# A two-layer hybrid decoder step on one core: the third token block's matmul operands made 128 rows high with zeros

## The chip, the cores and the metric

The kernel runs on one core of one Trainium2 chip. The metric is the device time of one execution in microseconds (us). Unchanged, it takes 1622.94 us, the median of three runs from 1620.73 to 1624.58.

## The reference

One inference step of a two-layer trunk on 256 prompt tokens and 64 sample tokens (8 sequences of 8), width 1024, all in float32. The kernel handles the 320 tokens in three blocks: 128, 128 and 64. Layer 0 mixes with four retention and four mLSTM heads and ends in a dense SwiGLU of width 2816; layer 1 mixes with eight HGRN2 heads and ends in two of eight SwiGLU experts. Cut to what matters here:

```python
def _retention(q, k, v, state):                      # per head and chunk
    intra = einsum('bhts,bhsv->bhtv', einsum('bhtk,bhsk->bhts', qc, kc) * decay, vc)
    inter = einsum('bhtk,bhkv->bhtv', qc, S) * q_dec
    S_new = S * chunk_dec + einsum('bhsk,bhsv->bhkv', kc * k_dec, vc)

def _mlstm(q, k, v, i_pre, log_f, C, n, m):
    s = einsum('bhtk,bhsk->bhts', qc, kc) * w
    num = einsum('bhts,bhsv->bhtv', s, vc) + w_prev[..., None] * einsum('bhtk,bhkv->bhtv', qc, C)
    den = sum(s, axis=-1) + w_prev * einsum('bhtk,bhk->bht', qc, n)
    n_new = dec[..., None] * n + einsum('bhsk,bhs->bhk', kc, w_end)

def _hgrn2(q, k, log_f, v, S):
    o = einsum('bhtk,bhkv->bhtv', qc * exp(A), S) + einsum('bhts,bhsv->bhtv', s, vc)

def _moe(h, w_router, b_router, wg, wu, wd):
    top_val, top_idx = top_k(einsum('bld,de->ble', h, w_router) + b_router, 2)
    gates = sum(one_hot(top_idx, 8) * softmax(top_val)[..., None], axis=-2)
    for e in range(8):
        out = out + gates[..., e:e + 1] * swiglu(h, wg[e], wu[e], wd[e])
```

## The kernel before

Each engine has its own instruction list, written in the order in which it runs, and semaphores tie the lists together. Activations are kept transposed, 128 features by 320 tokens. The mixers' order is written out by hand in two tables, `AB_STEPS` for layer 0 and `C_STEPS` for layer 1; every engine walks the same table and does its share of each step.

Where tokens have to be summed over, they lie on the partitions, and the three blocks of `BLK = [(0, 128), (128, 128), (256, 64)]` become three matmuls that contract over 128, 128 and 64 rows. Five places of that kind matter:

- `weigh` (L671 to L679), called by `outputs`: a head's values times the probabilities. L671 takes block 0, L672 block 1, L673 block 2 with 64 rows. Then come eight matmuls of 8 columns for the carried states (L679), or one against `ones` (L675) for the mLSTM denominator. It runs 20 times: 8 numerators and 4 denominators in layer 0, 8 numerators in layer 1. In some steps the pieces of a projection tile (L479 to L481) are woven between the state matmuls.
- `state_prompt` (L704 to L709): the new state of the prompt; L709 contracts the third block's keys over 64 rows against a mask of 8 columns, in four mLSTM heads.
- `state_samples` (L721): 32 rows high, eight instructions a head.
- `first_block` (L1046): gathers the tokens of expert 0's first round by a product of the token rows `HN` with a one-hot tile `ONE`, eight pieces of 128 features with three matmuls each, into two banks. ScalarE then rounds a bank to `xg_hi` (L1575), and VectorE computes the rest `xg_lo` (L2180).
- The loop over rounds follows. A round streams an expert's 35 weight units from HBM; ScalarE makes `w_hi` (L1568), VectorE `w_lo` (L2172), and TensorE multiplies (L479, L480, L481).

A float32 matmul in the program is two passes on the engine, each with a weight load (PEld) and a matmul (PE). So L673 is 40 of each in the trace and L1046 48 of each. Products in three float32r parts (L479 to L481) are one pass each.

Ahead of the loop VectorE's list has, in this order: the list of ranks and rows (to L2165), four units of `w_lo` (L2172), the gates (L2185 to L2193), and the two halves of `xg_lo` (L2180). `V` holds the values, `PB` and `PH` the probabilities of layer 0 and layer 1, `KN` the turned keys. All of these are regions of one large tile, `arena`, which the trace shows by that name; parts of it are used again for other things between the layers.

Of the kernel before, what the change touches and what calls it, by code (L numbers as in the profile page):

```python
# [15 lines left out]
P = 128  # L16
D = 1024
KD = D // P
TP = 256
NB, TS = 8, 8  # L20
SMP = NB * TS
NT = TP + SMP
BLK = [(0, 128), (128, 128), (256, 64)]
H4 = 4
HG = 8
DH = 128
# [23 lines left out]
CAP = 128  # L50
# [116 lines left out]
def trunk_kernel(nc, A, O):  # L167
    with ExitStack() as ctx:
# [5 lines left out]
        def S(name):  # L174
            if name not in sems:
                sems[name] = ctx.enter_context(nc.semaphore(name))
            return sems[name]

        banks = [ctx.enter_context(nc.psum_tensor(f"bank{i}", [P, 512], F32)) for i in range(8)]
# [23 lines left out]
        def C(name, rows=P):  # L203
            a, w = CONST[name]
            return cst[0:rows, a:a + w]
# [10 lines left out]
        ones = C("ones")  # L216

        def region(at, *shape):
            n = math.prod(shape)
            v = arena[:, at:at + n]  # L220
            if len(shape) == 1:
                return v
            if len(shape) == 2:
                return v.rearrange("p (a b) -> p a b", b=shape[1])
            return v.rearrange("p (a b c) -> p a b c", b=shape[1], c=shape[2])
# [6 lines left out]
        V = region(7680, 3, D)  # L232
# [5 lines left out]
        PB = region(21168, 2, 448)  # L238
# [11 lines left out]
        PH = region(23296, HG, 448)  # L250
# [22 lines left out]
        HN = region(4096, 3, D)  # L273
# [56 lines left out]
        WPS = small[:, 296:424].rearrange("p (a b) -> p a b", b=SMP)  # L330
# [33 lines left out]
        RTOK = sb("RTOK", [P, 3])  # L364
        HS = rows[0:KD, 0:2, :]
        XSQ = region(4352, D)
        ONE = region(8960, 3, CAP)

        DST = [ring[:, i * UNIT:(i + 1) * UNIT] for i in range(DSTAGE)]
        DWH = [parts(f"dense_hi_{i}", AT_RING + (DSTAGE + 2 * i) * UNIT, UNIT) for i in range(DSPLIT)]  # L370
# [74 lines left out]
        def _(pe):  # L445
            mm = nc.tensor.matmul
# [184 lines left out]
            for k in range(KD):  # L631
                b = open_bank("dve")
                for i, (t0, tn) in enumerate(BLK):
                    ins = nc.tensor.transpose(b[:, t0:t0 + tn], XN[0:tn, i, k * P:(k + 1) * P], ident[0:tn, 0:tn])
                close_bank("dve", ins, ("xT", k))
                if k == 3:
                    pe.wait_ge(S("prm_in"), 16 * 8)
                    b = open_bank("act")
                    ins = nc.tensor.transpose(b[:, 0:NPRM], PN[0:NPRM, :], ident[0:NPRM, 0:NPRM])
                    close_bank("act", ins, "prm")  # L640
            pe.wait_ge(S("token_scales"), 1)
            b = open_bank("dve")
            for i, (t0, tn) in enumerate(BLK):
                ins = mm(b[:, t0:t0 + tn], RS[0:tn, i:i + 1].to_broadcast([tn, P]), ident[0:tn, 0:tn], start=True, stop=True)
            close_bank("dve", ins, "n0_scale")
            pe.wait_ge(S("carry_in"), 32)
            b = open_bank("act")
# [21 lines left out]
            def weigh(b, left, probs, right, states, name, kind="dve"):  # L669

                mm(b[:, 0:TP], left(0), probs[:, 0:TP], start=True, stop=False, skip_group_check=True)  # L671
                mm(b[:, P:TP], left(1), probs[:, TP:TP + P], start=False, stop=False, skip_group_check=True)  # L672
                mm(b[:, TP:NT], left(2), probs[0:SMP, 384:448], start=False, stop=False, skip_group_check=True)  # L673
                if states is None:
                    ins = mm(b[:, TP:NT], ones, right, start=False, stop=True, skip_group_check=True)  # L675
                else:
                    yield
                    for s in range(NB):
                        ins = mm(b[:, TP + s * TS:TP + (s + 1) * TS], states[:, s, :], right[:, s * TS:(s + 1) * TS],  # L679
                                 start=False, stop=(s == NB - 1), skip_group_check=True)  # L680
                        if s % 2 and s < NB - 1:
                            yield
                close_bank(kind, ins, name)
                yield

            def outputs(layer, u, probs, probs_ready, right):
                values = lambda i: V[0:BLK[i][1], i, u * DH:(u + 1) * DH]
                probs_ready()
                pe.wait_ge(S(f"qe{layer}"), u // 4 + 1 if layer else u + 1)
                pe.wait_ge(S(f"state_in_{layer}_{u % NST}"), 16 * (u // NST + 1))  # L690
                kind = "act" if layer else "dve"
                b = open_bank(kind)
                yield from weigh(b, values, probs, right, ST[:, u % NST], ("num", layer, u), kind)
                if layer == 0 and u >= H4:
                    b = open_bank("dve")
                    pe.wait_ge(S("qn"), u - H4 + 1)
                    yield from weigh(b, lambda i: ones[0:BLK[i][1], :], probs, WPS[:, u % 2, :], None, ("den", u))

            def state_prompt(layer, u):
                after_empty(pe, ("kn", layer, u))  # L700
                kn = KN[:, u % 2]
                v = lambda i: V[0:BLK[i][1], i, u * DH:(u + 1) * DH]
                b = open_bank("act")
                mm(b[:, 0:DH], kn[:, 0, :], v(0), start=True, stop=False)  # L704
                ins = mm(b[:, 0:DH], kn[:, 1, :], v(1), start=False, stop=True)
                if layer == 0 and u >= H4:
                    mm(b[:, DH:DH + 1], kn[:, 0, :], ones[:, 0:1], start=True, stop=False)
                    mm(b[:, DH:DH + 1], kn[:, 1, :], ones[:, 0:1], start=False, stop=True)
                    ins = mm(b[:, DH + 1:DH + 9], kn[0:SMP, 2, :], C("bmask", SMP), start=True, stop=True)  # L709
                close_bank("act", ins, ("sp", layer, u))  # L710

            def state_samples(layer, u):
# [326 lines left out]
            def first_block():  # L1039

                pe.wait_ge(S("first_slots"), 3)
                for g in range(2):
                    for m in range(4):
                        at = slice((4 * g + m) * P, (4 * g + m + 1) * P)
                        for i, (t0, tn) in enumerate(BLK):
                            ins = mm(banks[g][:, m * CAP:(m + 1) * CAP], HN[0:tn, i, at], ONE[0:tn, i, :],  # L1046
                                     start=(i == 0), stop=(i == 2))
                    ins.then_inc(S("xg_full"), 1)

# [586 lines left out]
        def _(dve):  # L1636
# [15 lines left out]
                return bank_of(kind, n)  # L1652

            held = {"kind": "dve"}
            v.memset(rows[:, :, :], 0.0).then_inc(S("rows_zero"), 1)
            v.memset(wprow[:, :], 0.0).then_inc(S("rows_zero"), 1)

# [258 lines left out]
            def mix(src, tag, out, lo):  # L1916

                for u in range(KD):
                    if u == 2:
                        head_reciprocals(tag, 1)  # L1920
                    if u in HEADS[1]:
                        if tag == "hn1":
                            dve.wait_ge(S("gated1"), u + 1)
                        else:
                            after_empty(dve, ("cen", u))
                        scaled_head(src, tag, u)
                    low(out, u, src, lo)

            def projected_out(kind, tag, row, dst, lo=None, hi=None):
                for k in range(KD):  # L1930
                    add_to_x((kind, k), k)
                    after_empty(dve, (kind, k))
                    gained(tag, row, k, dst)
                    if k > 0 and lo is not None:
                        low(tag, k - 1, dst, lo, hi)
                    if k % 2:
                        split_dense()
                if lo is not None:
                    low(tag, KD - 1, dst, lo, hi)
                scale_of(tag)  # L1940
# [13 lines left out]
            for f in range(FT + 1):  # L1954
                if f < FT:
                    b = take(("fg", f))
                    free(v.tensor_tensor(SG[:, f % NSG, :], b[:, 0:NT], rsq[:, :], ALU.mult))
                if f == FT // 2:
                    for i in range(NST):
                        dve.wait_ge(S(f"state_out_{i}"), 16 * len(range(i, KD, NST)))  # L1960
                if f > 0:
                    dve.wait_ge(S("ff_hi"), f)
                    v.tensor_tensor(FTL[:, f - 1, :], SG[:, (f - 1) % NSG, :], FTH[:, f - 1, :].bitcast(F32),
                                    ALU.subtract).then_inc(S("ff_ready"), 1)
                if f < FT:
                    split_dense()
                    b = take(("fu", f))
                    dve.wait_ge(S("ff_silu"), f + 1)
                    free(v.tensor_tensor(SG[:, f % NSG, :], SG[:, f % NSG, :], b[:, 0:NT], ALU.mult))
# [71 lines left out]
            for name, u in C_STEPS:  # L2041
# [14 lines left out]
                elif name == "forget":  # L2056
                    forget(u)
                elif name == "scan":
                    dve.wait_ge(S("forget_ln"), u + 1)
                    for h in range(4):  # L2060
                        ins = v.tensor_tensor_scan(CUM[:, 4 * u + h, :], C("reset"), LV[u][1][:, h, :], 0.0, ALU.mult, ALU.add)
# [44 lines left out]
                                           op0=ALU.mult, op1=ALU.mult).then_inc(S("gated1"), 1)  # L2106
            after_fill(dve, ("lv", 1, 0))
            mix(OH, "hn1", "mix1", HL_O)
            projected_out("oc", "n3", 8, U_R)
            b = take("logit_rows")  # L2110
            dve.wait_ge(S("router_in"), 32)
# [277 lines left out]
```

## Time and profile before

| | before |
|---|---|
| median of 3 runs | 1622.94 us (1620.73 to 1624.58) |
| the profiled execution: time | 1626.39 us |
| its span, first to last instruction | 1624.6 us |
| TensorE busy | 1544.8 us, 95% |
| VectorE busy | 1167.6 us, 72% |
| ScalarE busy | 930.9 us, 57% |
| TensorE's mean granted clock | 0.965 of full |

The profiled execution is 3.45 us above the median of the runs, and its time is 1.8 us above its span. Busy TensorE time includes overlap of a pass with the next, so a stall of a tenth of a microsecond between passes can lie inside a stretch that counts as busy; it shows in the starts of the instructions.

### The profile page before, as it was taken

What the parts mean: (1) busy time and instruction counts of PE and PEld (TensorE: products, weight loads), DVE (VectorE), ACT (ScalarE), POOL (GpSimd) and SP (SyncE); (2) the same over time, 40 slices, a digit from 0 to 9 for tenths busy, and PEclk for the clock granted to TensorE, in tenths of its full rate; (3) what the DMA queues carried; (4) which work ended last, traced back from release to release, by engine and by line L of the source; (5) the groups of instructions that cost most, each with busy time, mean ns of one, the idle gap of its engine ahead of it and who ended that gap; (6) DMA issues with size and microseconds to landing.
All of it is one profiled execution on the core that took longest, in us unless ns stands there. A gap on an engine that the chain in (4) does not pass through costs nothing.

```text
span 1624.6 us, 23265 instructions
## 1 busy us (share of the span) xinstructions
PE 1544.8 (95%) x8656; PEld 1350.5 (83%) x8656; DVE 1167.6 (72%) x1256; ACT 930.9 (57%) x920; POOL 76.9 (5%) x90
## 2 busy tenths in 40 slices
PE   7999989999999989999989999999999999999994
PEld 5799778999999879986868888888888888888883
DVE  4755566555445696654468888888988888898887
ACT  4434544433334543333257786877778687777865
POOL 0012100000000000201020000000000000000001
PEclk9989999999999999977979999999999999999997
DMA  8567524797455422433189999999999999999983
GB/s 223 132 127 138 114 82 101 218 298 221 129 151 169 128 78 79 137 117 97 33 341 339 378 391 353 391 349 405 369 378 393 351 394 350 403 368 384 391 318 124
DMA packets 215874, 403.87 MB, mean 249 GB/s; under 512 B 15763, under 2 KB 132799, under 8 KB 215682
## 3 DMA queue, kind: packets, MB, share of 16 engines
q1 hardware_dynamic: 204400, 372.89, 66.7%
q0 software_dynamic: 6208, 22.06, 4.4%
q10 hardware_dynamic: 5202, 8.03, 1.5%
q8 instruction: 44, 0.72, 0.2%
q14 instruction: 20, 0.16, 0.0%
HBM read 372.65 MB, written 30.28 MB: 248 GB/s over the span
## 4 chain that ended last, share of the span: by engine, by line
PE 82%; DVE 8%; ACT 4%; issue 3%; DMA 2%; POOL 0%; ACTq 0%; SPq 0%; POOLq 0%; DVEq 0%
PE bank L479 24%; PE bank L480 23%; PE bank L481 23%; PE bank L679 2%; PE bank L936 1%; DVE dense_lo L1669 1%; PE bank L1075 1%; DVE w_lo L2172 1%; ACT dense_hi L1273 1%; PE bank L1046 1%; ACT w_hi L1568 1%; PE bank L721 1%; PE bank L584 1%; PE bank L671 1%; DVE arena L1778 1%
## 5 line engine op out<-in xcount | busy, mean ns | idle before, releaser
L2172 DVE TENSOR_TENSOR w_lo<-arena,w_hi 128x2048 fp32r<-128x2048 f32 (+1 forms) x284 | 606.4, 2169 | 104.0 <-ACT w_hi L1568 102.8
L1568 ACT ACTIVATE w_hi<-arena 128x2048 fp32r<-128x2048 f32 (+1 forms) x284 | 507.7, 1820 | 131.1 <-PE bank L481 118.6
L479 PE MATMUL bank<-w_hi,xg_hi 128*128 128x512 f32 (+1 forms) x768 | 288.0, 375 | 6.1 <-DVE w_lo L2172 4.7
L1669 DVE TENSOR_TENSOR dense_lo<-ring,dense_hi 128x2048 fp32r<-128x2048 f32 (+1 forms) x78 | 167.9, 2153 | 166.5 <-ACT dense_hi L1273 166.4
L480 PE MATMUL bank<-w_lo,xg_hi 128*128 128x512 f32 (+1 forms) x768 | 286.6, 373 | 0.0
L481 PE MATMUL bank<-w_hi,xg_lo 128*128 128x512 f32 (+1 forms) x768 | 285.8, 372 | 0.0
L1273 ACT ACTIVATE dense_hi<-ring 128x2048 fp32r<-128x2048 f32 (+1 forms) x78 | 140.6, 1803 | 161.1 <-PE bank L481 139.7
L479 PE MATMUL bank<-h_hi,dense_hi 128*128 128x320 f32 x512 | 171.9, 336 | 13.2 <-DVE h_lo_a L1675 5.2
L479 PEld LDWEIGHTS bank<-w_hi,xg_hi 128*128 128x128 f32 x768 | 144.9, 189 | 35.1 <-DVE w_lo L2172 7.6
L481 PEld LDWEIGHTS bank<-w_hi,xg_lo 128*128 128x128 f32 x768 | 144.5, 188 | 26.0
L480 PEld LDWEIGHTS bank<-w_lo,xg_hi 128*128 128x128 f32 x768 | 144.9, 189 | 25.0
L481 PE MATMUL bank<-h_hi,dense_lo 128*128 128x320 f32 x512 | 161.3, 315 | 0.0
L479 PE MATMUL bank<-w_hi,at_hi 128*128 128x512 f32 x352 | 139.3, 396 | 0.0
L481 PE MATMUL bank<-w_hi,at_lo 128*128 128x512 f32 x352 | 137.3, 390 | 0.0
L480 PE MATMUL bank<-w_lo,at_hi 128*128 128x512 f32 x352 | 137.0, 389 | 0.0
L479 PEld LDWEIGHTS bank<-h_hi,dense_hi 128*128 128x128 f32 x512 | 99.6, 195 | 24.4 <-issue 8.4
L479 PE MATMUL bank<-h_hi_f,dense_hi 128*128 128x320 f32 x352 | 109.5, 311 | 2.0 <-DVE h_lo_f L1675 1.9
L480 PE MATMUL bank<-h_lo_f,dense_hi 128*128 128x320 f32 x352 | 108.8, 309 | 0.0
L481 PE MATMUL bank<-h_hi_f,dense_lo 128*128 128x320 f32 x352 | 108.8, 309 | 0.0
L481 PEld LDWEIGHTS bank<-h_hi,dense_lo 128*128 128x128 f32 x512 | 99.5, 194 | 0.0
L480 PE MATMUL bank<-h_lo_a,dense_hi 128*128 128x320 f32 x256 | 81.4, 318 | 0.0
L481 PEld LDWEIGHTS bank<-w_hi,at_lo 128*128 128x128 f32 x352 | 66.1, 188 | 14.1
(391 smaller groups left out, 2376.4 us busy)
## 6 DMA issues: line engine op xcount, KB each, us to landing
arena<-in_w_moe_down SPq DMA_DIRECT2D x176, 512.0 KB, 6.3
arena<-in_w_moe_gate SPq DMA_DIRECT2D x128, 512.0 KB, 6.9
arena<-in_w_moe_up SPq DMA_DIRECT2D x128, 512.0 KB, 6.7
arena<-in_w_moe_gate SPq DMA_DIRECT2D x64, 384.0 KB, 4.1
arena<-in_w_moe_up SPq DMA_DIRECT2D x64, 384.0 KB, 3.8
ring<-in_w_in_ab SPq DMA_DIRECT2D x32, 512.0 KB, 9.0
ring<-in_w_in_c SPq DMA_DIRECT2D x32, 512.0 KB, 4.7
expert_rows<-ZERO SPq DMA_DIRECT2D x12, 1024.0 KB, 7.5
```

The source lines that it names most:

```text
L479: mm(out, left[0], right[0], start=start, stop=False)
L480: mm(out, left[0], right[1], start=False, stop=False)
L481: return mm(out, left[1], right[0], start=False, stop=stop)
L584: ins = mm(b[:, 0:NT], C("inv_d"), SQF[tag][:, k, :], start=(k == 0), stop=(k == KD - 1))
L671: mm(b[:, 0:TP], left(0), probs[:, 0:TP], start=True, stop=False, skip_group_check=True)
L679: ins = mm(b[:, TP + s * TS:TP + (s + 1) * TS], states[:, s, :], right[:, s * TS:(s + 1) * TS], start=False, stop=(s == NB - 1), skip_grou ...
L721: ins = mm(b[:, h * 256:(h + 1) * 256].rearrange("p (b v) -> p b v", v=DH), kn[rows_g, 2, :], VX[rows_g, at, :], start=True, stop=True)
L936: ins = mm(b[:, (2 * q + i) * P:(2 * q + i + 1) * P], L[:, h + q, at], L[:, h + q, at], start=True, stop=True)
L1273: fn(unit_flat(n, DWH), unit_flat(n, DST), ACT.Copy).then_inc(S("dense_hi"), 1)
L1568: fn(WH[SLOT_OF[p]][:, 0:unit_size(p)], STAGE[:, s, 0:unit_size(p)], ACT.Copy).then_inc(S("unit_hi"), 1)
L1669: v.tensor_tensor(unit_flat(n, DWL), unit_flat(n, DST), unit_flat(n, DWH).bitcast(F32), ALU.subtract).then_inc(S("dense_split"), 1)
L2172: v.tensor_tensor(WL[w][:, 0:n], STAGE[:, s, 0:n], WH[w][:, 0:n].bitcast(F32), ALU.subtract).then_inc(S("unit_split"), 1)
```

## The change

The third block's operands are taken 128 rows high in `weigh`, `outputs`, `state_prompt` and `first_block`. Rows 64 to 127 of the values, the probabilities, the token rows and the one-hot tile are set to zero by memsets on VectorE, so that the sums stay the same. The constant mask `bmask` already has zeros there. `state_samples`, the scores and the transposes stay as they were. `ONE` moves to another address, since the old one is still in use when its rows are set to zero.

```diff
-        ONE = region(8960, 3, CAP)
+        ONE = region(10240, 3, CAP)
...
-                mm(b[:, TP:NT], left(2), probs[0:SMP, 384:448], start=False, stop=False, skip_group_check=True)
+                mm(b[:, TP:NT], left(2), probs[:, 384:448], start=False, stop=False, skip_group_check=True)
...
             def outputs(layer, u, probs, probs_ready, right):
-                values = lambda i: V[0:BLK[i][1], i, u * DH:(u + 1) * DH]
+                values = lambda i: V[:, i, u * DH:(u + 1) * DH]
...
-                    yield from weigh(b, lambda i: ones[0:BLK[i][1], :], probs, WPS[:, u % 2, :], None, ("den", u))
+                    yield from weigh(b, lambda i: ones, probs, WPS[:, u % 2, :], None, ("den", u))
...
-                    ins = mm(b[:, DH + 1:DH + 9], kn[0:SMP, 2, :], C("bmask", SMP), start=True, stop=True)
+                    ins = mm(b[:, DH + 1:DH + 9], kn[:, 2, :], C("bmask"), start=True, stop=True)
...
                         for i, (t0, tn) in enumerate(BLK):
-                            ins = mm(banks[g][:, m * CAP:(m + 1) * CAP], HN[0:tn, i, at], ONE[0:tn, i, :],
+                            ins = mm(banks[g][:, m * CAP:(m + 1) * CAP], HN[:, i, at], ONE[:, i, :],
                                      start=(i == 0), stop=(i == 2))
...
+            def pad_values():
+                v.memset(V[SMP:P, 2, :], 0.0)
+
+            pad_values()
+            v.memset(PB[SMP:P, :, 384:448], 0.0)
             v.memset(rows[:, :, :], 0.0).then_inc(S("rows_zero"), 1)
...
                 if f == FT // 2:
+                    v.memset(PH[SMP:P, :, 384:448], 0.0)
...
                 elif name == "scan":
+                    if u == 0:
+                        pad_values()
                     dve.wait_ge(S("forget_ln"), u + 1)
...
             mix(OH, "hn1", "mix1", HL_O)
+            v.memset(HN[SMP:P, 2, :], 0.0)
+            v.memset(ONE[SMP:P, 2, :], 0.0)
             projected_out("oc", "n3", 8, U_R)
```

No instruction of TensorE, ScalarE, GpSimd or SyncE is added, dropped or moved; VectorE's list gets six memsets. Where they stand is seen in three pieces. Lines below the diff's first insertion carry higher numbers after it. The first piece is VectorE's list in layer 1 where the eight values are padded again, just ahead of the first scan (L2061 before, L2070 after); first the kernel before:

```order
L1990 TENSOR_SCALAR arena<-arena 128x320
L2047 TENSOR_TENSOR arena<-bank3,rsq 128x320
L1669 TENSOR_TENSOR dense_lo_0_71<-ring,dense_hi_0_69 128x2048
L2061 SCALAR_TENSOR_TENSOR arena<-cst,arena 128x320 x4
L1998 TENSOR_TENSOR arena<-arena 128x4x128
```

And the same place of the changed kernel:

```order
L1997 TENSOR_SCALAR arena<-arena 128x320
L2054 TENSOR_TENSOR arena<-bank3,rsq 128x320
L1675 TENSOR_TENSOR dense_lo_0_71<-ring,dense_hi_0_69 128x2048
L1657 MEMSET arena 64x1024
L2070 SCALAR_TENSOR_TENSOR arena<-cst,arena 128x320 x4
L2005 TENSOR_TENSOR arena<-arena 128x4x128
```

One memset of 64 rows by 1024 columns has come in between the split of a weight unit and the scan; nothing else moved.

The second piece is VectorE's list at the end of layer 1's mixer, behind the last head's `h_lo_o` and ahead of the first sum into `xT` (L1690 before, L1696 after). Before:

```order
L1849 TENSOR_TENSOR arena<-arena,bank2 128x320
L1675 TENSOR_TENSOR h_lo_o_54<-arena,h_hi_51 128x320
L1690 TENSOR_TENSOR xT<-xT,bank3 128x320
L1680 TENSOR_SCALAR cst<-xT,prm 128x320
L1690 TENSOR_TENSOR xT<-xT,bank4 128x320
```

After:

```order
L1855 TENSOR_TENSOR arena<-arena,bank2 128x320
L1681 TENSOR_TENSOR h_lo_o_54<-arena,h_hi_51 128x320
L2118 MEMSET arena 64x1024
L2119 MEMSET arena 64x128
L1696 TENSOR_TENSOR xT<-xT,bank3 128x320
L1686 TENSOR_SCALAR cst<-xT,prm 128x320
```

The memsets of the token rows and of the one-hot tile have come ahead of the first sum into `xT`.

TensorE's list at the first `weigh` reads the same in both kernels, since such a row shows the output's shape (128 by 64 for the third block) and not the height of the operands:

```order
L671 MATMUL bank5<-arena 128x256
L672 MATMUL bank5<-arena 128x128
L673 MATMUL bank5<-arena 128x64
L679 MATMUL bank5<-small,arena 128x8 x8
L658 MATMUL bank6<-arena 128x256
```

Only the height of L673's operands differs, 64 rows before and 128 after.

## Rows read from the trace of the kernel before

**Rows 1.** The page: TensorE's busy line, and the chain that ended last, by engine.
```profile
PE 1544.8 (95%) x8656; PEld 1350.5 (83%) x8656; DVE 1167.6 (72%) x1256; ACT 930.9 (57%) x920; POOL 76.9 (5%) x90
...
PE 82%; DVE 8%; ACT 4%; issue 3%; DMA 2%; POOL 0%; ACTq 0%; SPq 0%; POOLq 0%; DVEq 0%
```

**Rows 2.** Stage; us; busy (x) of PE, PEld, DVE, ACT, POOL; PE clock; DMA share; GB/s.
```profile
85.00:250.00 165.00, 154.16 (x968) 132.32 (x966) 100.51 (x222) 74.80 (x146) 28.33 (x39) 0.95 0.54 110
635.00:780.00 145.00, 139.59 (x858) 121.89 (x857) 85.81 (x171) 45.64 (x72) 19.35 (x20) 0.82 0.36 109
825.00:841.00 16.00, 14.88 (x48) 11.22 (x48) 12.15 (x19) 10.37 (x9) 8.62 (x6) 0.50 1.00 377
841.00:1600.00 759.00, 754.01 (x3611) 630.60 (x3612) 652.90 (x391) 575.26 (x422) 4.90 (x3) 1.00 0.96 365
```

**Rows 3.** Timeline of the gather's weight loads: start, us, instruction, form, count [idle before].
```profile
824.82 0.93 PEld L1046 LDWEIGHTS bank<-arena 128*128 128x128 f32 x4 [3.04 <-DVE RND L2160]
825.97 0.50 PEld L1046 LDWEIGHTS bank<-arena 64*128 64x128 f32 x2 [0.23 <-issue]
826.70 0.93 PEld L1046 LDWEIGHTS bank<-arena 128*128 128x128 f32 x4 [0.22 <-issue]
```

**Rows 4.** Timeline of TensorE at one `weigh` of layer 0, full clock.
```profile
100.53 0.38 PE L672 MATMUL bank<-arena 128*128 128x128 f32 x2
100.85 0.43 PE L673 MATMUL bank<-arena 64*128 64x64 f32 x2
101.21 1.95 PE L679 MATMUL bank<-small,arena 128*128 128x8 f32 x16
103.02 0.40 PE L479 MATMUL bank<-h_hi,dense_hi 128*128 128x320 f32 x1
```

**Rows 5.** The same at a `weigh` of layer 1 at half clock.
```profile
725.52 0.63 PE L672 MATMUL bank<-arena 128*128 128x128 f32 x2
...
726.71 2.09 PE L679 MATMUL bank<-arena 128*128 128x8 f32 x9
```

**Rows 6.** The chain in order of time: state matmuls behind `weigh`, and the gather.
```profile
87.13 1.88 PE bank L679 x16
...
720.63 3.51 PE bank L679 x16
...
753.63 3.51 PE bank L679 x16
```

**Rows 7.** VectorE and ScalarE at places where the chain leaves TensorE (timeline).
```profile
138.09 0.68 DVE L1778 SCALAR_TENSOR_TENSOR arena<-arena,bank 128x128 f32<-128x128 f32 x3 [1.15 <-PE bank L721]
...
709.09 0.49 DVE L2047 TENSOR_TENSOR arena<-bank,rsq 128x320 f32<-128x320 f32 x1 [0.94 <-PE bank L481]
```

**Rows 8.** Timeline of VectorE and ScalarE at the end of the gather.
```profile
839.24 0.69 DVE L2180 TENSOR_TENSOR xg_lo<-bank,xg_hi 128x512 fp32r<-128x512 f32 x1
840.55 0.69 DVE L2180 TENSOR_TENSOR xg_lo<-bank,xg_hi 128x512 fp32r<-128x512 f32 x1 [0.62 <-ACT xg_hi L1575]
...
835.01 0.58 ACT L1575 ACTIVATE xg_hi<-bank 128x512 fp32r<-128x512 f32 x1
839.92 0.60 ACT L1575 ACTIVATE xg_hi<-bank 128x512 fp32r<-128x512 f32 x1 [4.33 <-PE bank L1046]
```

**Rows 9.** VectorE where memsets come in (timeline): start, layer 1's scan, first sum.
```profile
1.22 1.66 DVE L1655 MEMSET rows<- 128x1920 f32 x1 [1.22 <-PEq L2381]
...
553.71 2.97 DVE L2061 TENSOR_TENSOR_SCAN arena<-cst,arena 128x320 f32<-128x320 f32 x4 [2.07 <-ACT arena L1518]
...
784.37 0.49 DVE L1690 TENSOR_TENSOR xT<-xT,bank 128x320 f32<-128x320 f32 x1 [0.81 <-PE bank L481]
```

**Rows 10.** VectorE at the start and in the dense SwiGLU (timeline).
```profile
9.99 0.49 DVE L1694 COPY xT<-bank 128x320 f32<-128x320 f32 x1 [7.03 <-PE bank L634]
...
380.31 2.29 DVE L1669 TENSOR_TENSOR dense_lo<-ring,dense_hi 128x2048 fp32r<-128x2048 f32 x1 [3.32 <-ACT dense_hi L1273]
```

**Rows 11.** Busy time and clock after the loop's start (windows).
```profile
846.00:850.00 4.00, 4.00 (x19) 3.31 (x18) 2.29 (x1) 3.19 (x2) 0.00 (x0) 1.00 0.05 18
```

## The prediction

> **What bounds the kernel now.** The page comes first: TensorE is busy for 95% of the span, and 82% of the chain that ended last is TensorE's [rows 1]. Then the busy time by stage. In both mixers and in the expert loop TensorE is busy for 93 to 99% of the stage. The gather ahead of the loop is the odd one: 48 passes fill 14.9 of 16 us, at a granted clock of 0.50, that is 1.2 GHz instead of 2.4 [rows 2]. The expert loop, 759 us, holds none of the changed matmuls.
>
> Next, the starts of the instructions around a change of height. In the gather, four loads with 128 rows follow each other inside 0.93 us, so each begins while the matmul before it runs. Then the engine's load side idles for 0.23 us, two loads with 64 rows come, and it idles for 0.22 us before the next with 128 rows [rows 3]. Columns, outputs and clock are the same on both sides; only the height differs. So a load whose height is not that of the matmul ahead waits until that matmul has drained, and one of the same height does not. The same is seen at the third block of `weigh` [rows 4, 5].
>
> **The gather, on TensorE.** One piece of 128 features is six passes, and the first two pieces begin at 824.82 and 826.70, 1.88 us apart [rows 3]; eight of them are the 15 us of the stage. A pass without a switch at this clock: 16 passes of the state matmuls take 3.51 us where they run without one [rows 6], 0.22 us each, so six are 1.32 us. That removes 0.56 us a piece, 4.4 us over eight pieces. The stage is then about 10.5 us instead of 15, and less if the denser work brings the clock up.
>
> **The gather, on the path.** Almost none of this reaches the end, because VectorE is late next. Its list has the weight parts and the gates ahead of `xg_lo`; it comes to the first half at 839.24 and to the second at 840.55, of which 0.62 us was a wait for ScalarE's second `xg_hi`, which had waited 4.33 us for the gather [rows 8]. With an early gather ScalarE does both halves back to back from 835.01 and is done by 836.2, and VectorE's second half follows its first without a gap. VectorE then ends about 0.65 us earlier, and so does the loop's start. Nothing else ahead of it depends on the gather. **Term: 0.65 us** (bounds: 0 if VectorE is held up elsewhere, 4.4 if I misread its list).
>
> **weigh, on TensorE.** From the first pass of L672 to the first of L679 are four passes: 0.68 us at full clock [rows 4]. Sixteen passes of L679 take from 101.21 to 103.02, 0.113 us each [rows 4]; four are 0.45 us, so 0.23 us goes. The pass behind the second switch starts slowly as well, which may add 0.02; I take 0.24. At half clock it is 1.19 us [rows 5] against 4 times 0.22, so 0.31 us goes. In the gather two loads with 64 rows fill 0.50 us and four with 128 rows 0.93 us [rows 3], which is one pace for both, 0.21 us for each further load; so the added rows cost no load time.
>
> There are 20 calls. In the chain, nine of the ten unwoven groups of 16 state matmuls appear, from 87.13 to 753.63 [rows 6], and the chain is on TensorE at the ten woven calls too; one call lies beside it. Three of the 19 on the chain run at half clock: there the 16 passes take 3.51 us instead of 1.88 [rows 6]. So 16 times 0.24 plus 3 times 0.31 is **4.8 us**. L709 switches from 128 to 64 rows and then to the 32 of L721; only the first switch goes, three of these four stand off the chain, and I put 0.1 us for all. L721's own switches stay.
>
> **How much of it passes.** Where the chain leaves TensorE, the other engine had been waiting for it: 0.94 and 1.15 us at the two tightest such places that I found [rows 7]. The matmul stretches between two such places hold two to four calls, 0.5 to 1.0 us of saving, just inside those waits. But the profile does not show waits that are nearly binding, and after a saving ScalarE's or VectorE's own list may be what ends some of them. I let 0.6 of the 4.9 us be lost: **4.3 us** passes (bounds: 2.0 and 4.9).
>
> **The memsets.** One of 128x1920 took 1.66 us, 0.86 ns a column [rows 9]; half the partitions may or may not be faster, and I take the same per column. The two at the program's start (1024 and 128 columns, 1.0 us) lie in the 7.03 us in which VectorE waits for the first transposes [rows 10]. The one in the dense SwiGLU (512 columns, 0.44 us) falls into a stage where VectorE waits 3.3 us in each step for a weight part [rows 10]. The one ahead of the scan (0.88 us) has 2.07 us of wait for ScalarE to fill [rows 9]. The two behind the mixer (1.0 us) stand where VectorE waits 0.81 us before the first sum [rows 9]; 0.2 us is not covered there, but TensorE has its next projection tiles to go on with. I cost all six at nothing. If none of this cover held, they would cost 3.3 us together.
>
> **The sum.** 4.3 + 0.65 is 5.0 us. Against the profiled execution of 1626.39 us that is 1621.4; it lies 3.45 us above the median of the runs, which would become 1617.9. I say **1618.0 us**, 0.31% below 1622.94. A difference of 0.2%, 3.2 us, is about what a measurement of this kernel can tell from no change.
>
> **Rival: the stalls go, the time stays (0.2).** Each saving is a quarter of a microsecond, and each could be eaten by the next wait. For it speaks that 18% of the chain is not TensorE's [rows 1] and that the largest single saving, the gather's, is already hidden. Against it the waits of 0.94 us and more at those places [rows 7]. With half the savings passed, 2.5 us, the time is 1620.5.
>
> **Rival: the height is not the cause (0.07).** Then the gaps stay and the time is 1623. What speaks for it: in `weigh` the number of columns changes too. What speaks against it: in the gather only the height changes [rows 3]. The Trainium skill ("TensorE: Matmul & The Clock Gate", section Part 3, "What overlaps and what doesn't") says that weight loads overlap running matmuls only when the row groups differ. By that rule 128-high operands behind 128-high ones could not overlap either, padding would remove nothing, and the sum would be zero. The trace does not agree: loads with 128 rows overlap each other there.
>
> **Rival: the clock turns it around (0.06), slower.** In the gather TensorE has only half the clock [rows 2], and has all of it by 846, 5 us into the loop [rows 11]. If the gather ends some 5 to 8 us earlier, the engine is idle until 840.6, and what the loop starts with could be a clock that comes back later than before. Each microsecond at half clock costs the loop half a microsecond. From 10 us more on, the 5.0 us are used up; with another 16 us like those of the gather [rows 2] the loss is 8 us, and the time is 1626. Against it: TensorE has no more waits in the loop than before, and in this trace the clock came back within 5 us of the loop's start, from an equally low state [rows 11].
>
> **A better case (0.1).** With the stalls gone, some of the stretches at half clock in layer 1 could go too. The stage's mean of 0.82 over 145 us means 52 us at half clock [rows 2], and a fifth less would give back 5 us: 1613.
>
> **How the numbers follow.** The forecast has 0.57, for 1616.4 to 1619.6. The range must take in the better case and most of the rival with half the savings: 1613.5 to 1622.0, which leaves out about 0.2 (the unchanged time, the slow clock, and the edge of the better case). Faster by over 0.2% means below 1619.7: the forecast and the better case give 0.67. Within 0.2% lie the half savings and the unchanged time, 0.27. Slower 0.06.
>
> **What would show it.** In the changed trace L1046's loads all have 128 rows and no idle time between them; 48 passes take 10.5 us or less. L672 to L679 take 0.45 us at full clock. ScalarE's two `xg_hi` stand back to back, the two halves of `xg_lo` do too, and the first L479 of the loop comes 0.65 us earlier in relation to VectorE's gates, with TensorE idle before it for 5 us or more. The expert loop looks as before. The prediction is wrong if the starts of passes in `weigh` still lie 0.68 us apart, if TensorE's waits in the mixers grow by what the passes lost, or if the stretches at half clock change by more than 5 us in sum.

## The result, and the profile after

The changed kernel took 1605.01 us (median of four runs, 1604.51 to 1605.55), before 1622.7 (four runs). The ratio is 0.9889 with a 95% interval of 0.9873 to 0.9905: 18 us less, where about 5 were forecast. In two later sets of rounds the same kernel came to 0.9905 and 0.9914, so 14 to 18 us is what it gains.

The page of the changed kernel: busy time, the granted clock in 40 slices, and the chain by engine.

```profile
PE 1516.5 (95%) x8656; PEld 1331.4 (83%) x8656; DVE 1171.1 (73%) x1262; ACT 931.1 (58%) x920; POOL 77.0 (5%) x90
...
PEclk9999989999999999988989999999999999999997
...
PE 81%; DVE 9%; ACT 4%; issue 3%; DMA 2%; POOL 0%; ACTq 0%; SPq 0%; POOLq 0%; DVEq 0%
```

The clock line of the kernel before, which was not shown ahead of the prediction:

```profile
PEclk9989999999999999977979999999999999999997
```

TensorE's share is that of [rows 1] and its part of the chain within one per cent of it, but TensorE is busy for 28 us less with the same 8656 passes. The clock lines say where to look: slices 3, 18, 19 and 21 of before are lower. Slice 6 is lower in the changed kernel, so the low places also move.

The stages of the changed kernel (same columns as [rows 2]), cut where the same work begins and ends: layer 0's mixer, layer 1's, the gather, the expert loop.

```profile
85.00:241.80 156.80, 146.45 (x968) 127.33 (x966) 100.51 (x222) 74.85 (x146) 29.40 (x39) 0.97 0.57 116
627.00:758.50 131.50, 125.00 (x854) 110.08 (x854) 85.84 (x171) 45.67 (x72) 19.38 (x20) 0.91 0.39 121
803.30:819.10 15.80, 8.07 (x49) 7.88 (x49) 12.47 (x20) 11.07 (x9) 8.63 (x6) 0.72 1.01 379
819.10:1578.00 758.90, 754.20 (x3614) 630.86 (x3615) 653.01 (x390) 574.92 (x421) 3.79 (x3) 1.00 0.96 365
```

Against [rows 2] layer 0's mixer is 8.2 us shorter and layer 1's 13.5; that is more than the 18 us of the medians because the profiled execution of before was a long one. VectorE's and ScalarE's busy times in them are the same to 0.1 us. The mean clock rose from 0.95 to 0.97 and from 0.82 to 0.91. The gather's stage is as long as before (15.8 against 16.0 us), since VectorE ends it, as forecast; TensorE's 48 passes fill 8 us of it instead of 15. The loop is the same.

TensorE's timeline at the `weigh` of [rows 4], in the changed kernel:

```profile
97.07 0.38 PE L672 MATMUL bank<-arena 128*128 128x128 f32 x2
97.29 0.33 PE L673 MATMUL bank<-arena 128*128 128x64 f32 x2
97.46 1.90 PE L679 MATMUL bank<-small,arena 128*128 128x8 f32 x16
```

From L672 to L679 it takes 0.39 us instead of 0.68: 0.29 us less, where 0.24 was forecast. A call of layer 1 at half clock, for [rows 5]:

```profile
709.10 0.63 PE L672 MATMUL bank<-arena 128*128 128x128 f32 x2
...
709.85 1.82 PE L679 MATMUL bank<-arena 128*128 128x8 f32 x8
```

Here it is 0.75 us instead of 1.19: 0.44 us less, where 0.31 was forecast. The weight loads of the gather, as in [rows 3]:

```profile
803.29 7.84 PEld L1046 LDWEIGHTS bank<-arena 128*128 128x128 f32 x48 [3.05 <-DVE RND L2171]
819.06 0.29 PEld L479 LDWEIGHTS bank<-w_hi,xg_hi 128*128 128x128 f32 x1 [7.92 <-DVE xg_lo L2191]
```

The 48 loads are one row now: no idle time between them, 7.84 us instead of 15. The first 4.7 us of them ran at a granted clock of 0.50 and the last 3.2 at 0.94 (windows). Behind them TensorE's load side waits 7.92 us for VectorE. ScalarE's and VectorE's rows at that place (timeline), for [rows 8]:

```profile
813.49 1.07 ACT L1575 ACTIVATE xg_hi<-bank 128x512 fp32r<-128x512 f32 x2
```

```profile
815.57 0.17 DVE L2196 TENSOR_TENSOR GATE<-GATE,arena 128x24 f32<-128x24 f32 x1
...
817.72 1.29 DVE L2191 TENSOR_TENSOR xg_lo<-bank,xg_hi 128x512 fp32r<-128x512 f32 x2
```

Both halves of `xg_hi` and of `xg_lo` stand back to back. VectorE is through with `xg_lo` 1.29 us after it begins, where before it took from 839.24 to 841.24: about 0.7 us less. The memsets, again on VectorE's timeline (start, before layer 1's scan, behind the mixer):

```profile
1.02 0.91 DVE L1657 MEMSET arena<- 64x1024 f32 x1 [1.02 <-PEq L2392]
...
543.69 0.91 DVE L1657 MEMSET arena<- 64x1024 f32 x1 [0.27 <-issue]
545.49 2.97 DVE L2070 TENSOR_TENSOR_SCAN arena<-cst,arena 128x320 f32<-128x320 f32 x4 [0.89 <-ACT arena L1518]
...
762.30 0.91 DVE L2118 MEMSET arena<- 64x1024 f32 x1 [0.27 <-issue]
763.19 0.17 DVE L2119 MEMSET arena<- 64x128 f32 x1
763.37 0.49 DVE L1696 TENSOR_TENSOR xT<-xT,bank 128x320 f32<-128x320 f32 x1
```

0.91 us each for 1024 columns; the scan still waits 0.89 us for ScalarE behind its memset.

So the savings that were counted out are there, and add up to about 6 us. The other 8 to 12 us need another source, and the clock lines point at the clock. One stretch as an example. First the kernel before, then the changed one, both from 88 to 112 us (windows, columns as above):

```profile
88.00:112.00 24.00, 24.00 (x137) 21.48 (x137) 12.52 (x31) 9.71 (x22) 3.58 (x8) 0.79 0.55 90
```

```profile
88.00:112.00 24.00, 23.56 (x167) 21.69 (x167) 17.70 (x43) 11.43 (x29) 5.19 (x9) 1.00 0.70 129
```

In the same 24 us the changed kernel makes 167 passes instead of 137. In the kernel before, one call of `weigh` lies in it and another call's third block just ahead of it, together worth 0.6 us of stalls. The clock was 0.79 of full and is 1.00. One stretch of one execution proves little, though: the same window is looked at in other runs below (e4).

### The profile page after: what moved, and what is told of

Its sections match the earlier page's. It is cut to its first block, busy times and chain, and to the rows that moved or that the text cites. A ratio compares the mean times of both kernels' runs of the same rounds, so it can differ in the third digit from the quotient of the medians.

```text
span 1602.7 us, 23271 instructions
## 1 busy us (share of the span) xinstructions
PE 1516.5 (95%) x8656; PEld 1331.4 (83%) x8656; DVE 1171.1 (73%) x1262; ACT 931.1 (58%) x920; POOL 77.0 (5%) x90
## 4 chain that ended last, share of the span: by engine, by line
PE 81%; DVE 9%; ACT 4%; issue 3%; DMA 2%; POOL 0%; ACTq 0%; SPq 0%; POOLq 0%; DVEq 0%
PE bank L479 24%; PE bank L480 23%; PE bank L481 23%; DVE w_lo L2183 2%; PE bank L679 2%; DVE dense_lo L1675 1%; PE bank L936 1%; PE bank L1075 1%; ACT dense_hi L1273 1%; ACT w_hi L1568 1%; PE bank L721 1%; PE bank L584 1%; DVE arena L1784 1%; PE bank L671 1%; PE bank L616 1%
```

## The experiments

The theory: each stall of a height change is short, but the stalls stand among thin matmuls (8 columns), and without them TensorE spends less time at the lower clock level (0.50 of full in the traces). The rival A: stalls alone, with the surplus from somewhere else (the gather, the memsets, the address of `ONE`). The rival B: it is the height of the third block itself, not the stalls, that the clock follows. In the expectations "Theory A" is the clock theory each time; "Theory B" is whatever other account that text names.

A measure for all runs is the time at half clock, 2 x (1 - clock) x span. It is given for the profiled execution and, since every execution's span and clock are known, as the mean of all runs. The second counts: within one kernel the executions differ by 6 us or so (standard deviation). Some 20 us of it in each run lie at the kernel's end.

| run | median us | ratio to before, interval | profiled span | clock | at half clock | the same, mean of all runs (runs) |
|---|---|---|---|---|---|---|
| before | 1622.7 | | 1624.6 | 0.965 | 114 | 107, 112, 109 (25, 19, 13) |
| changed | 1605.0 | 0.9889 (0.9873 to 0.9905) | 1602.7 | 0.976 | 77 | 77 (4) |
| e1, layer 0 alone | 1618.8 | 0.9972 (0.9952 to 0.9991) | 1620.6 | 0.965 | 113 | 102 (9) |
| e2, layer 1 alone | 1613.5 | 0.9935 (0.9905 to 0.9964) | 1615.1 | 0.970 | 97 | 90 (5) |
| e3, gather alone | 1621.9 | 0.9998 (0.9979 to 1.0018) | 1618.7 | 0.970 | 97 | 101 (10) |
| e4, before with added work | 1628.1 | 1.0041 (1.0023 to 1.0058) | 1624.4 | 0.972 | 91 | 98 (10) |
| e5, changed with switches | 1623.2 | 0.9994 (0.998 to 1.0008) | 1626.2 | 0.968 | 104 | 98 (10) |
| e6, changed, states too | 1609.9 | 0.9893 (0.987 to 0.9915) | 1609.1 | 0.977 | 74 | 67 (4) |
| e7, memsets alone | 1624.1 | 0.9993 (0.9982 to 1.0004) | 1623.6 | 0.963 | 120 | 111 (10) |
| e8, changed again | 1611.4 | 0.9905 (0.9887 to 0.9923) | 1610.2 | 0.971 | 93 | 87 (4) |
| e9, changed, control of e5 | 1612.3 | 0.9935 (0.9915 to 0.9956) | 1610.0 | 0.975 | 81 | 81 (6) |
| e10, changed, added work | 1612.6 | 0.995 (0.9932 to 0.9967) | 1610.0 | 0.974 | 84 | 79 (8) |
| e11, changed again | 1608.1 | 0.9914 (0.9886 to 0.9942) | 1609.8 | 0.972 | 90 | 80 (4) |

The kernel before had medians of 1620.49 beside e1 to e4, 1625.24 beside e5 to e8 and 1622.72 beside e9 to e11, with single runs from 1617 to 1628. So ratios are compared, not medians of different sets. These 57 runs also give the price of the clock, for they are one program, and their time at half clock goes from 97 to 124 us: a run with 1 us more of it is 0.38 us longer (the slope inside the three sets; 95% interval 0.32 to 0.43).

**e1, e2 and e3: the change in parts.** Each takes one part of the diff onto the kernel before: e1 the layer-0 half of `outputs` with `V` and `PB` set to zero, e2 the layer-1 half, e3 `first_block` with its two memsets.

```diff
-                values = lambda i: V[0:BLK[i][1], i, u * DH:(u + 1) * DH]
+                values = lambda i: V[0:(P if layer == 0 else BLK[i][1]), i, u * DH:(u + 1) * DH]
```

(and `layer == 1` in e2.)

> Only layer 0's weigh (8 numerators, 4 denominators) takes the third block 128 rows high; everything else as before. Theory A (clock): the passes saved at 12 switches are 12 times 0.29 = 3.5 us, and the two stretches at half clock before 110 us (10.2 us in the profile of before) go as well, which gives up to 5 us more: 8 us less than before in all, 1614.5. Theory B (stalls alone, the rest of the change's gain is from layer 1 or from elsewhere): 3.5 us less, 1619.

> Only layer 1's weigh (8 numerators) is 128 rows high. Theory A (clock): 8 switches pairs times 0.3 = 2.4 us, and some 20 us of half clock between 600 and 780 us go, worth 8 us more: 1612. Theory B (stalls alone): 2.4 us less, 1620.3. If the two layers add up, this run and the one of layer 0 together give the change's gain less 0.6 us for the gather.

> Only the gather of the first round is 128 rows high, with its two memsets. Both theories: the gather takes about 8 us instead of 15, the loop's start comes 0.65 us earlier in relation to VectorE's gates, the time is 0.65 us less, inside the noise: 1622. A rival that puts the change's surplus here (a loop that starts with a better clock) expects 5 us or more.

Measured: 0.28%, 0.65% and 0.02% less, that is 4.5, 10.5 and 0.3 us, in sum 15.4 us, as much as the whole change in e8. The eight calls of layer 1 gave more than twice what the twelve of layer 0 gave, with stalls worth only 2.4 us. e2 fits the clock theory (10.4 us) and not the stalls alone (2.4): its interval is 6 to 15 us, and it has 17 us less at half clock than before (90 against 107). e1 lies between 3.5 and 8, and its interval of 1.5 to 8 us doesn't decide; it has 5 us less at half clock. e3 takes the gather out as a source of 5 us or more: its 48 passes are done early, and the time is the same to within 3.4 us either way. It does have 6.5 us less at half clock (101 against 107). Its trace has 14 us of it around the gather where before had 20, a place where TensorE waits for VectorE anyway, so this part buys no time.

**e7: the memsets alone.** The changed kernel with all operands back at 64 rows.

> The six memsets and the moved one-hot tile of the change, with every matmul as before. All theories: the memsets lie in VectorE's waits and cost nothing, so the time is that of before within the noise. If they cost their own length it is 3.3 us more.

Ratio 0.9993, interval 0.9982 to 1.0004: nothing that can be told from no change. The memsets cost less than 1 us, and no more than 3 us of the gain can be theirs or the new address's. The time at half clock is that of before as well (111 against 112). With e3 this ends rival A as the source of the 8 to 12 us.

**e4: work added to the kernel before.** Two matmuls among the state matmuls of each numerator call:

```diff
                     for s in range(NB):
+                        if s in (0, 4):
+                            mm(b[:, NT:512], states[:, s, :], cst[:, CONST["cos"][0]:CONST["cos"][0] + 192],
+                               start=False, stop=False, skip_group_check=True)
                         ins = mm(b[:, TP + s * TS:TP + (s + 1) * TS], states[:, s, :], right[:, s * TS:(s + 1) * TS],
```

> The kernel before with all its 64-row matmuls, and two added matmuls of 192 columns per numerator call of weigh, into bank columns that nobody reads (16 calls, 32 matmuls, 64 passes of about 0.16 us at full clock, 10 us of work added; the result is unchanged). Theory A (clock): the added work fills the thin place behind the switches, the stretches at half clock in the mixers shrink from 75 us in sum to under 50, and the time rises by less than the 10 us added, or even falls: 1618 to 1628. Theory B (the clock has nothing to do with it): low stretches as before and about 9 to 10 us more, 1632.

The time rose by 0.41%, 6.6 us, for 10 us of added work: less than the work, as the clock theory had it. The median of 1628.06 is at the edge of that theory's range. The other account's 9 to 10 us lie at the upper end of the interval, 3.7 to 9.4 us. The clock decides more clearly: 98 us at half clock against 107 in the same rounds, 9.3 less (95% interval 3.5 to 15). At 0.38 us each that gives back 3.5 us, and 10 less 3.5 is what was measured. The window from 88 to 112 us of this run:

```profile
88.00:112.00 24.00, 24.00 (x168) 21.88 (x167) 14.25 (x31) 11.05 (x29) 5.13 (x10) 1.00 0.65 104
```

With all stalls left in, this stretch is at 1.00 instead of 0.79. But it is not fixed to one value either way. The same window of e3, which has all the stalls in layer 0, then of e9 (below), which has none:

```profile
88.00:112.00 24.00, 24.00 (x158) 22.07 (x158) 15.67 (x36) 11.07 (x28) 3.84 (x8) 0.93 0.64 118
```

```profile
88.00:112.00 24.00, 23.75 (x147) 21.30 (x147) 14.64 (x32) 10.98 (x27) 3.63 (x7) 0.86 0.57 92
```

Over all thirteen profiles: 0.79 in four with the stalls in layer 0 (before, e2, e5, e7) and 0.93 in e3; 1.00 in six without them (changed, e1, e6, e8, e10, e11) and 0.86 in e9; 1.00 in e4. So the stalls make the low place likely and do not settle it alone. With e4 the account is that the clock goes with how thickly TensorE's work lies; how it is granted in detail is not shown here.

**e5 and e9: the switches put back, and their control.** The changed kernel with one small matmul ahead of the third block in every call, 64 rows high in e5 and 128 in e9. The third block stays 128 rows high in both.

```diff
+                mm(b[:, NT:NT + 8], left(2)[0:SMP], probs[0:SMP, 384:392], start=False, stop=False, skip_group_check=True)
                 mm(b[:, TP:NT], left(2), probs[:, 384:448], start=False, stop=False, skip_group_check=True)
```

(e9 has `left(2), probs[:, 384:392]`.)

> The changed kernel, and in every weigh call one added matmul 64 rows high and 8 columns wide ahead of the third block, into bank columns that nobody reads; the result is unchanged. It brings back the two switches of height per call, while the third block itself stays 128 rows high. Direct cost: two passes of 0.11 us and 0.3 us of stalls, 20 calls, about 10 us. Theory A (the stalls are what costs the clock): the stretches at half clock in the mixers grow back towards the 75 us of before, and the time rises by more than the direct cost, to 1618 to 1626. Theory B (the clock follows the height of the third block's operands): low stretches stay near 44 us and the time is 1615.

> The control of the switch run: the changed kernel with the same added matmul of 8 columns per weigh call, but 128 rows high, so that the work is added and no switch. Direct cost: two passes of 0.11 us, 20 calls, 4.4 us. Theory A (the stalls cost the clock): the stretches at half clock in the mixers stay where the changed kernel has them (44 and 58 us in its two profiles), against 72 us in the switch run, and the time is 2 to 5 us above the changed kernel, 1608 to 1614. Theory B (any thin added matmul lowers the clock): low stretches and time as in the switch run, 1620 or more.

TensorE's timeline at one call of e5 (its L673 is the added matmul, L674 the third block, L680 the states):

```profile
102.50 0.38 PE L672 MATMUL bank<-arena 128*128 128x128 f32 x2
102.81 0.39 PE L673 MATMUL bank<-arena 64*128 64x8 f32 x2
103.13 0.43 PE L674 MATMUL bank<-arena 128*128 128x64 f32 x2
103.40 0.79 PE L680 MATMUL bank<-small,arena 128*128 128x8 f32 x6
```

And at the same call of e9:

```profile
100.09 0.38 PE L672 MATMUL bank<-arena 128*128 128x128 f32 x2
100.31 0.29 PE L673 MATMUL bank<-arena 128*128 128x8 f32 x2
100.45 0.41 PE L674 MATMUL bank<-arena 128*128 128x64 f32 x2
100.71 0.45 PE L680 MATMUL bank<-small,arena 128*128 128x8 f32 x3
```

0.90 us against 0.62 from L672 to L680: the same matmuls, and 0.28 us more only because one of them has another height. The weight loads of the added matmul, in e5 and then in e9, show it on the load side:

```profile
102.81 0.29 PEld L673 LDWEIGHTS bank<-arena 64*128 64x128 f32 x2
```

```profile
100.20 0.30 PEld L673 LDWEIGHTS bank<-arena 128*128 128x128 f32 x2
```

The first comes 0.31 us after the start of L672's matmuls, the second 0.11 us.

e5 is back at the time of before (0.9994), e9 kept most of the gain (0.9935). The added matmul itself has a part in that: e9 is 0.21%, 3.4 us, above e11, the changed kernel in the same rounds, near the 4.4 us expected. The height is the difference between e5 and e9, 0.59%, 9.6 us; the stalls on the path are 19 x 0.28 = 5.3 us of it. The two intervals are 0.14% and 0.2% wide to a side, so the rest, 4 us, is not certain from the times alone. The clock is clearer. e5 has 98 us at half clock (ten runs), 15 less than the kernel before in its rounds; e9 has 81 (six runs), 28 less than before in its own. That puts 13 us on the height (95% interval 7 to 19), worth 5 us at 0.38 each. The windows of e5, then of e9, from 600 to 680 us, in which layer 1's first `weigh` calls lie (e5 is some 9 us further back in its program there, so the work is not quite the same):

```profile
600.00:680.00 80.00, 72.75 (x551) 69.30 (x551) 57.43 (x108) 27.81 (x34) 7.70 (x6) 0.89 0.27 83
```

```profile
600.00:680.00 80.00, 75.46 (x605) 72.61 (x604) 58.18 (x111) 28.27 (x38) 11.83 (x10) 0.95 0.36 108
```

From 700 to 780 us it is 0.79 against 0.85. Rival B falls: the third block is 128 rows high in both, and with the stalls back more than half of the half-clock time that the change took from the mixers is back. In the traces the mixers have 72 us of it in e5 and 48 in e9, against 75, 65 and 78 in before, e3 and e7.

**e8 and e11: the changed kernel again.**

> The changed kernel once more, on the chip and in the rounds of these experiments, since the kernel before spread over 1617 to 1628 us here. If the result holds, it is 15 to 18 us below before.

> The changed kernel in the same rounds, to compare these two with: 13 to 18 us below the kernel before. Its stretches at half clock in the mixers are 40 to 60 us if the earlier two profiles were typical.

Both held, at 15 and 14 us. Their runs have 87 and 80 us at half clock on average, those of the first result 77, so the first result was the best of three.

**e6 and e10: is there more to have?** e6 pads `state_samples` as well, so that no height changes in the mixers' state work; e10 puts one added matmul of 192 columns per call into the changed kernel.

```diff
-        VX = region(14592, NB // 2, DH)
+        VX = region(14592, NB, DH)
...
-                        ins = mm(b[:, h * 256:(h + 1) * 256].rearrange("p (b v) -> p b v", v=DH), kn[rows_g, 2, :],
-                                 VX[rows_g, at, :], start=True, stop=True)
+                        ins = mm(b[:, h * 256:(h + 1) * 256].rearrange("p (b v) -> p b v", v=DH), kn[:, 2, :],
+                                 VX[:, at, :], start=True, stop=True)
```

> The changed kernel, and state_samples 128 rows high as well: eight column groups of values masked to their sequence instead of four, GpSimd's masking twice as wide. Trace of after: 16 heads have a switch from 128 to 32 rows and back, about 0.6 us of stalls at full clock, but the two 32-row groups also run side by side (8 passes of 256 columns in 1.07 us instead of 8 times 0.21). Direct effect: zero within 2 us. Theory A (the clock follows the stalls): fewer low stretches, 3 to 8 us less than the changed kernel, 1597 to 1602. Theory B: the time of the changed kernel, 1605.

> The changed kernel with one added matmul of 192 columns per numerator call among the state matmuls (16 calls, 5 us of work, result unchanged). If added dense work still buys clock once the stalls are gone, the low stretches in the mixers fall from about 50 us to 35 or less and the time falls by up to 3 us against the changed kernel of the same rounds. If what is left at half clock comes from waits for other engines, they stay near 50 and the time rises by 5 us.

e6 has the least time at half clock of all, 67 us in the mean, and yet 0.9893 against 0.9905 of e8 in the same rounds: the same within the intervals. The 3 to 8 us that the clock theory expected of it did not come. Its eight state passes no longer run side by side: at one head of layer 0 they take 1.89 us where they took 1.14. With 16 heads that can use up what the clock gave; that it did is not shown by a run of its own. e10 has 79 us against 80 in e11 and is 0.36% slower, 5.8 us, about its added work of 5 us. With the switches gone, added work bought nothing that these runs can show. Neither beats the changed kernel.

## Why the prediction was wrong

**The cause of the stalls: right.** A load whose height differs from that of the matmul ahead starts only about when that one is done (0.31 us behind its start, against 0.11); e5 and e9 show it with the height as the only difference. The rival that the height is not the cause falls. So does the rule that the prediction quoted for it from the Trainium skill ("TensorE: Matmul & The Clock Gate", Part 3, "What overlaps and what doesn't"), as far as these loads go: in the changed kernel 48 loads of 128 rows behind matmuls of 128 rows ran without idle time between them.

**The gather: right.** It took 7.84 us of loads (10.5 or less was forecast, "less if the denser work brings the clock up", which it did for the last 3.2 us), the loop started about 0.7 us earlier in relation to VectorE's gates (0.65), and TensorE waited for VectorE before it for 7.92 us ("5 us or more"). e3 found no measurable gain in it.

**weigh, on TensorE: a little small.** 0.29 us a call at full clock where I took 0.24. I gave every pass behind L672 the pace of the thin state passes, 0.113 us, and in the changed trace the four take 0.39 us. Over 19 calls this is 5.5 us instead of 4.8, and 6.0 with three calls at the 0.44 us that one at half clock saved.

**How much of it passes: nearly all, as far as the sum below shows.** No run measures it alone. VectorE's and ScalarE's busy times are unchanged stage by stage, and TensorE's nine largest waits for them from 85 to 780 us add up to 25 us before and 26 after.

**The memsets: right.** e7 leaves less than 1 us for them.

**The clock: the step that failed.** The sum is 4.3 us of stalls plus 0.65 us of the gather, with the clock at nothing. I had the mechanism, but only as "A better case (0.1)": "some of the stretches at half clock in layer 1 could go too", "a fifth less would give back 5 us". That was wrong in four ways. It was given one chance in ten when it was the likely course: every profile of the changed kernel shows fewer such stretches in the mixers (44, 58 and 55 us against 75, 65 and 78 in before, e3 and e7). It was looked for in layer 1 alone, while layer 0 had a low place as well, from 88 to 112 us, and lost it in all three. Its size was too small: in the first profile layer 1's stage has 24 us at half clock left of 52. And it was left out of the forecast's sum. The prediction's own sign of being wrong, "if the stretches at half clock change by more than 5 us in sum", came true.

The account, from all runs in the rounds of e8 and e11: the changed kernel's spans are 14 us shorter in the mean in both, with 26 and 29 us less at half clock. Some 6.5 of these are the gather's and buy nothing (e3), so about 20 are left. At the 0.38 us found inside the runs of the kernel before, they are worth 8 us; half a microsecond each would be the most, since half the clock is half the pace (3.51 us for the 16 passes that take 1.88 at full clock). The 6 us of stalls and gather make it 14. So the missing term measures about 8 us, more than the whole forecast of 5, and the range's lower end, 1613.5, was too high because of it.

**The slower rival** did not come: behind a 7.92 us wait the loop took 758.9 us, as long as before (759.0).

Why the twelve runs of the changed kernel have anything from 71 to 93 us at half clock is left open; it differs from execution to execution, and times with it.

## What to carry to other kernels

In a float32 stream of small matmuls, keep the operands' height the same from one to the next, with zeros if need be: a change to 64 rows and back costs 0.29 us at full clock here, and a full-height load takes no longer than a half-height one (0.19 us each). When TensorE's clock stands at half in a stage, price a small edit there twice: once for the stalls it removes, and once for the half-clock time that they may hold in place, with up to half of that time as the upper end of the range (each microsecond was worth 0.38 us in this kernel). And before taking credit for a large local saving, as the gather's 7 us here, read what the next engine's list has ahead of the work that takes up the result.

## What the runs showed of the hardware that was not expected

Stalls of 0.3 us per call, among passes with 8 columns, went with 13 us more at half clock over a kernel of 1600 us (e5 against e9, which differ in the height of one matmul per call, each compared with the kernel before in its own rounds). 10 us of added, useless matmuls cost only 6.6 us, with 9 us less at half clock (e4). Within one unchanged kernel the time at half clock went from 97 to 124 us from execution to execution, and the span with it, 0.38 us for each. Two groups of matmuls 32 rows high ran beside each other (eight passes in 1.14 us); making them 128 rows high (e6, 1.89 us) took away the switches and gained nothing.
